# A four-layer hybrid decoder on one core: the first mixer's gate work moved one slot, more buffers, and its constants and first squares moved ahead

## The reference, cut to what matters

```python
def _rg_lru_mixer(h, w_in, conv_w, conv_b, w_gate, b_gate, lam, w_out):
    bsz, s, _ = h.shape
    proj = h @ w_in
    gate_branch, xr = proj[..., :D_RNN], proj[..., D_RNN:]
    xc = _causal_dwconv(xr, conv_w, conv_b)
    xb = xc.reshape(bsz, s, LRU_BLOCKS, LRU_BLK)
    gates = (jnp.einsum('bsnc,nce->bsne', xb, w_gate) + b_gate).astype(jnp.float32)
    r = jax.nn.sigmoid(gates[..., :LRU_BLK]).reshape(bsz, s, D_RNN)
    i = jax.nn.sigmoid(gates[..., LRU_BLK:]).reshape(bsz, s, D_RNN)
    log_a = -LRU_C * r * jax.nn.softplus(-lam.astype(jnp.float32))
    a = jnp.exp(log_a)
    u = jnp.sqrt(-jnp.expm1(2.0 * log_a)) * (i * xc.astype(jnp.float32))
    _, hs = lax.associative_scan(_linear_combine, (a, u), axis=1)
    y = jax.nn.gelu(gate_branch.astype(jnp.float32)) * hs
    return y.astype(h.dtype) @ w_out
```

## Time and profile before

| | us |
|---|---|
| median of three runs (1874.1 to 1875.57) | 1874.65 |
| the profiled execution | 1872.53 |
| its span, first to last instruction | 1870.7 |
| mean granted clock of TensorE, as a share | 0.988 |

### The profile page before, as it was taken

One profiled execution on the slowest core, in us unless ns is written; L12 is line 12 of the kernel. 1 busy time (PEld: TensorE's weight loads), 2 busy tenths in 40 slices (PEclk: granted clock), 3 DMA queues, 4 the chain that ended last, 5 costly groups with the idle time before them and its releaser, 6 DMA issues.

```text
span 1870.7 us, 25413 instructions
## 1 busy us (share of the span) xinstructions
PE 1798.5 (96%) x8912; PEld 1131.2 (60%) x8912; DVE 1194.5 (64%) x1971; ACT 1143.2 (61%) x1601; POOL 1178.1 (63%) x1678
## 2 busy tenths in 40 slices
PE   6989999999999898999999999999999999999999
PEld 3545666655655555666666776666657777566665
DVE  6775777327877853777416875777137777577730
ACT  6876666557776745766545667666443545676642
POOL 4545877876354436777886307777875445478785
PEclk9999999999999998999999999999999999999999
DMA  5314444444223223444443103444442222244443
GB/s 203 109 57 147 136 154 143 153 148 129 80 79 91 80 68 113 157 147 147 145 157 115 58 2 119 151 147 141 160 133 90 81 89 76 83 150 144 152 155 120
DMA packets 64926, 224.80 MB, mean 120 GB/s; under 512 B 7328, under 2 KB 8864, under 8 KB 64544
## 3 DMA queue, kind: packets, MB, share of 16 engines
q1 hardware_dynamic: 64224, 221.69, 36.4%
q10 hardware_dynamic: 576, 1.49, 0.2%
HBM read 221.05 MB, written 2.10 MB: 119 GB/s over the span
## 4 chain that ended last, share of the span: by engine, by line
PE 78%; ACT 9%; DVE 9%; issue 3%; DMA 0%; POOL 0%; DVEq 0%; SPq 0%; ACTq 0%
PE psum L274 22%; PE psum L284 21%; PE psum L316 12%; PE psum L320 11%; PE psum L1657 3%; ACT w_big L232 2%; PE psum L1239 1%; PE psum L2051 1%; DVE psum L1463 1%; PE psum L2034 1%; PE psum L2070 1%; ACT x_big L342 1%; PE psum L1228 1%; ACT psum L1328 1%; ACT psum L346 1%
## 5 line engine op out<-in xcount | busy, mean ns | idle before, releaser
L248 POOL TENSOR_TENSOR w_rest<-w_panel,w_big 128x256 bf16<-128x256 f32 (+1 forms) x1674 | 1177.9, 742 | 679.7 <-ACT w_big L232 679.6
L274 PE MATMUL psum<-x_big,w_big 128*128 128x512 f32 x2248 | 662.8, 428 | 14.9 <-ACT x_big L342 14.3
L284 PE MATMUL psum<-x_rest,w_rest 128*128 128x512 bf16 x2248 | 556.8, 383 | 1.4 <-POOL w_rest L248 1.4
L232 ACT ACTIVATE w_big<-w_panel 128x1024 fp32r<-128x1024 f32 (+3 forms) x425 | 422.3, 1018 | 171.6 <-PE psum L320 93.2
L274 PEld LDWEIGHTS psum<-x_big,w_big 128*128 128x128 f32 x2248 | 420.0, 190 | 138.6 <-issue 20.0
L284 PEld LDWEIGHTS psum<-x_rest,w_rest 128*128 128x128 bf16 x2248 | 189.6, 98 | 284.2 <-issue 106.8
L605 DVE SCALAR_TENSOR_TENSOR psum<-ffn_raw,params,psum 128x512 f32<-128x512 f32 x352 | 264.5, 752 | 7.2 <-ACT psum L559 1.0
L597 DVE TENSOR_TENSOR ffn_raw<-psum,rstd 128x512 f32<-128x512 f32 x176 | 121.3, 691 | 141.2 <-PE psum L284 121.2
L559 ACT ACTIVATE psum<-ffn_raw,params 128x512 f32<-128x512 f32 x176 | 137.4, 782 | 101.5 <-DVE ffn_raw L597 101.3
L316 PE MATMUL psum<-g_big,w_big 128*128 128x512 f32 x704 | 199.3, 423 | 0.0
L451 DVE SCALAR_TENSOR_TENSOR x_resid<-psum,x_resid 128x512 f32<-128x512 f32 x64 | 43.8, 688 | 227.8 <-PE psum L320 227.7
(11 more groups left out here) (251 smaller groups left out, 1831.5 us busy)
## 6 DMA issues: line engine op xcount, KB each, us to landing
w_panel<-in_up SPq DMA_DIRECT2D x176, 512.0 KB, 3.4
w_panel<-in_dn SPq DMA_DIRECT2D x64, 448.0 KB, 3.1
w_panel<-in_ssd_in SPq DMA_DIRECT2D x41, 512.0 KB, 3.5
w_panel<-in_dn SPq DMA_DIRECT2D x32, 512.0 KB, 3.4
w_panel<-in_hgrn_in SPq DMA_DIRECT2D x32, 512.0 KB, 3.5
w_panel<-in_lru_in SPq DMA_DIRECT2D x19, 512.0 KB, 3.4
w_panel<-in_ssd_out SPq DMA_DIRECT2D x16, 512.0 KB, 3.5
w_panel<-in_swa_in SPq DMA_DIRECT2D x12, 512.0 KB, 3.5
```

The costliest lines, as they stand in the source:

```text
L232: act.activation(k.w1[:, slot, lo:words], k.w[:, slot, lo:words], ACT.Copy, scale=(SHIFT - 1) / SHIFT).then_inc(k.s("panel_big"), 1)
L248: rest = pool.tensor_tensor(k.w2[:, slot, a], k.w[:, slot, a], k.w1[:, slot, a].bitcast(F32), ALU.subtract)
L274: pe.matmul(out, k.w1[:, slot, q * m:(q + 1) * m], k.x1[:, q, :], start=q == 0, stop=False)
L284: mm = pe.matmul(out, k.w2[:, slot, q * m:(q + 1) * m], k.x2[:, q, :], start=False, stop=q == DT - 1)
```

## The change

- **The queues of the units.** The inner and GELU steps of unit j move into slot j+1, as `inner(j - 1)` and `gelu(j - 1)` on VectorE and `gelu(j - 1)` on ScalarE. ScalarE's square of gate j stays in slot j, at its end, ahead of the root, which now stands at the end of the even slots. `rest` moves from slot j+3 to slot j+4, right behind `raw`. `gates(0)` on TensorE comes ahead of gate tile 1.
- **Buffers.** `a`, `root` and `wu` have four, with waits on unit j-4. The order of the bank releases changes accordingly, and `release` says which comes when.
- **The last two units.** After slot 9 the steps of units 8 and 9 alternate, the y of unit 9 stands in bank 5, and `lru_step` counts the steps in the new order. TensorE takes unit 6, then unit 7, into the early output tiles before it waits for all ten.
- **Softplus.** `lru_lambda` is loaded with the first small DMA. The chain begins ahead of the tiles of x and ends behind them, before the units; two of its buffers are now in PSUM.
- **The head.** The squares of x tiles 1 to 5 are done by GpSimd, in two pieces of 128x256 each, ahead of its panels (the rest of panel 0 comes behind the first square). ScalarE runs an exponential on a dummy as its first operation. It rounds panel 1 before the norm and panel 2 behind it; before, it rounded panels 1 and 2 ahead of the norm.

```diff
+POOL_SQUARES = range(1, 6)
...
+def release(g):
+    if g >= 2 * LRU_T:
+        return g
+    j = g // 2
+    return min(g + 1, 2 * LRU_T - 1) if g % 2 else max(g - 1, 0)
@@ first_scalar
+    act.wait_ge(k.s("banks_free"), 4)
+    act.activation(b.t4, k.rstd[:, 0:LRU_T], ACT.Exp)
...
         scaled_x(act, k, 0, o)
-        square_x(act, k, 0, o)
-    round_until(act, k, 2)
+        if o == 0:
+            square_x(act, k, 0, o)
+            softplus_scalar(act, k, "lru_softplus", b.t3, b.t1)
+        elif o not in POOL_SQUARES:
+            square_x(act, k, 0, o)
+    round_until(act, k, 1)
+def first_squares(pool, k):
+    for o in POOL_SQUARES:
+        pool.wait_ge(k.s(f"x{o}_landed"), 16)
+        if o >= 3:
+            pool.wait_ge(k.s("sq_summed"), o - 2)
+        for half in range(2):
+            at = slice(half * PIECE, (half + 1) * PIECE)
+            sq = pool.tensor_tensor(k.sq[:, o % 2, at], k.x[:, o, at], k.x[:, o, at], ALU.mult)
+        sq.then_inc(k.s("x_squared_pool"), 1)
+        if o == 1:
+            weights_gpsimd(pool, k, 0)
@@ first_vector, behind the loop over the tiles of x
+    lru_softplus_end(dve, k, softplus)
@@ LruBuffers
-        self.conv, self.a, self.root, self.wu = (a.take(2, S) for _ in range(4))
+        self.conv = a.take(2, S)
+        self.a, self.root, self.wu = (a.take(4, S) for _ in range(3))
@@ lru_y
-    return k.ps[:, 7 if j % 2 else 4, :]
+    return k.ps[:, 5 if j == LRU_T - 1 else 7 if j % 2 else 4, :]
@@ lru_tensor
-        if j > 1:
-            gates(j - 1)
+        gates(j - 1)
         project(gate_tile(j))
-        if j == 1:
-            gates(0)
-    pe.wait_ge(k.s("lru_y_split"), LRU_BEGUN - 2)
-    out_steps(pe, k, "lru_out", 0, 0, LRU_BEGUN - 2, k.y1, k.y2)
+    out(0, 0, LRU_BEGUN - 2)
     gates(LRU_T - 1)
...
+    out(1, 0, LRU_BEGUN - 2)
+    for o in (2, 3):
+        out(o, 0, LRU_BEGUN - 1)
+    for o in (0, 1):
+        out(o, LRU_BEGUN - 2, LRU_BEGUN - 1)
+    for o in range(OUT_EARLY["lru_out"]):
+        out(o, LRU_BEGUN - 1, LRU_BEGUN)
@@ lru_scalar
+    for j in range(LRU_T):
+        bias(j)
+        round_ahead(act, k, job, raw_tile(j))
+        if j:
+            gates(j - 1)
+            decay(j - 1)
+        round_ahead(act, k, job, gate_tile(j))
+        if j:
+            gelu(j - 1)
+        if j >= 3:
+            high(j - 3)
+        square(j)
+        if j >= 2 and j % 2 == 0:
+            root(j - 2)
+    gates(LRU_T - 1)
+    decay(LRU_T - 1)
+    gelu(LRU_T - 1)
+    root(LRU_T - 2)
+    for j in range(LRU_T - 3, LRU_T):
+        high(j)
@@ lru_vector
+    for j in range(LRU_T):
+        mid, old = j >= 1, j >= 3
+        raw(j)
+        if j >= 4:
+            rest(j - 4)
+        tap(j, 0)
         if old:
             rooted(j - 3)
+        tap(j, 1)
         if old:
             driven(j - 3)
+        tap(j, 2)
         if old:
             scan(j - 3)
+        if mid:
+            gated(j - 1)
+            inner(j - 1)
         if old:
             joined(j - 3)
+        gate(j)
         if mid:
+            gelu(j - 1)
+    six, seven, eight, nine = range(LRU_T - 4, LRU_T)
+    rest(six)
+    inner(nine)
+    rooted(seven)
+    gated(nine)
+    driven(seven)
+    gelu(nine)
+    scan(seven)
+    joined(seven)
+    rooted(eight)
+    rooted(nine)
+    driven(eight)
+    driven(nine)
+    rest(seven)
+    scan(eight)
+    scan(nine)
+    joined(eight)
+    joined(nine)
+    rest(eight)
+    rest(nine)
```

More of the change, by code:

```diff
@@ L393, in sum_squares @@
         return
-    dve.wait_ge(k.s("x_squared"), DT * c + o + 1)
+    if c == 0 and o in POOL_SQUARES:
+        dve.wait_ge(k.s("x_squared_pool"), o)
+    else:
+        dve.wait_ge(k.s("x_squared"), x_squared(c, o))
     if o > 1:
@@ L685, in __init__ @@
         self.half_bias = a.take(2 * LRU_T)
-        self.nlam, self.t0, self.t1, self.t2, self.t3 = (a.take(LRU_T) for _ in range(5))
+        self.nlam, self.t0, self.t1, self.t2, self.t3, self.t4 = (a.take(LRU_T) for _ in range(6))
         self.gate_w = a.take(LRU_T * 256)
```

134 lines of the change are left out of this document (57 added, 77 removed).

## The result

The changed kernel takes 1850.99 us (median of four runs, 1850.15 to 1851.29), against 1874.38 for the kernel before, measured beside it (four runs, 1873.68 to 1875.57). The ratio is 0.9874, with a 95% interval from 0.9857 to 0.9891: 23.4 us won, where 22.6 were forecast. The profiled execution took 1850.15 us with a span of 1848.3, and the mean granted clock was 0.994 instead of 0.988.

The account below looks back on a forecast made before the run. TensorE, busy for 96% of the span, was taken as the bound, with VectorE and ScalarE waiting for each other inside mixer units; 2.5 + 6.7 + 7.8 + 5.6 = 22.6 us off 1874.65 gave 1852.0, range 1848.5 to 1861.0.

Parts of the forecast that it names:

- head, to unit 0: Start of the kernel: squares on GpSimd and an earlier table load start unit 0 at 24.5 against 26.98, 2.5 us.
- units 0 to 2: First mixer units: softplus chain out of slot 0, gates(0) ahead of gate tile 1; 22.9 us instead of 29.6, 6.7 won.
- units 3 to 8: Middle mixer units: reordered queues give 8.9 us even, 10.5 odd slots; 56.8 us against 64.6, 7.8 won.
- tail: From unit 9's start to the last rest: 24.1 us instead of 29.7, 5.6 us won.
- output tiles: Behind the last rest: 24.9 us that hang on the last high, which keeps its place; they stay.
- late next: Odd slots: the bias queued behind ScalarE's table load and root starts 2.35 us behind raw, so the slot takes 10.5 us.
- Slow squares: Head: GpSimd needs 1.46 us a piece, squares 2 to 5 end 5.8 us later, 1857.8 us; chance 0.12.
- The pair stays: Mixer units: reordering only moves the stall, table loads and bias wait remain, 7.8 us not won, 1859.8; chance 0.12.
- The clock: Unit gates: new TensorE idles halve its clock, 2.6 us each, 28.6 us in all, 1880.6; chance 0.03.
- The shared port: Seven units: GpSimd's pieces come before VectorE's rooted, which loses up to 0.73 us each, 5.1 us, 1857.1; chance 0.08.

Follow-up runs that it names:

- doubled squares: Changed kernel with GpSimd making each of its five squares of x tiles twice, the first copy to spare memory: 1854.57 us, ratio 0.9895.
- late softplus: Changed kernel with the end of the softplus chain back in VectorE's slot 0, behind the eviction of gate 0: 1851.69 us, ratio 0.9882.
- panel 2 first: Changed kernel with panel 2 rounded ahead of the norm again, nothing else moved: 1851.87 us, ratio 0.9873.
- root's table removed: Changed kernel with a copy of the same shape in place of the square root, so the units need no table loads: 1848.80 us, ratio 0.9862.
- bias moved: Changed kernel with the bias of units 5, 7 and 9 on VectorE instead of ScalarE: 1847.37 us, ratio 0.9852.
- GELU in its own slot: Changed kernel with inner, gelu and bank release back in the unit's own slot, gated and rest in old places, four buffers kept: 1864.86 us, ratio 0.9946.
- serial tail: Changed kernel with units 8 and 9 one after the other on VectorE instead of alternating: 1852.17 us, ratio 0.9877.

## Why the prediction was right, step by step

The walk through the queues carried it. The forecast of 1852.0 lies between the two medians of the changed kernel, 1850.99 and 1852.74, so the last microsecond of the agreement means nothing. Its five terms, each from the traces of before and of the changed kernel:

| step | forecast | measured |
|---|---|---|
| head, to unit 0 | 2.5 | 26.98 - 24.25 = 2.7 |
| units 0 to 2 | 6.7 | 29.57 - 23.57 = 6.0 |
| units 3 to 8 | 7.8 | 64.61 - 56.34 = 8.3 |
| tail | 5.6 | 29.73 - 23.96 = 5.8 |
| output tiles | 0 | -0.1 to 0.1 |
| sum, to the FFN | 22.6 | 22.7 |

*Head.* The total was right, one of its reasons was wrong, and two errors covered each other. I had priced a piece of a square at 0.73 us and called GpSimd's squares the pace of the head. The source line's summary in the changed kernel (ns, least, median, most):

```profile
L415 POOL TENSOR_TENSOR x_sq<-x_resid x10: 608/620/1161, 7.2 to 14.5; 128x256 f32<-128x256 f32 x10
```

The eight pieces of squares 2 to 5 take 4.62 us together, 0.58 each, and end at 15.14 where I had 16.2. The pace is ScalarE's: two operations for a tile, 1.23 us apart from 8.97 on, with no idle between them. The doubled squares show how near GpSimd is behind. The last sum ended at 18.4 instead of 19.4, but in TensorE's queue the sum over features stands behind the remainders of tile 0, eight matmuls in 3.64 us from 16.97, and started at 20.40. So raw 0 came at 24.25, almost as forecast (24.5).

*Units 0 to 2* were over-estimated by 0.7 us. The walk had the queues of the changed kernel right; what it named as the reasons of the gain, the chain out of slot 0 and `gates(0)` ahead, is in part not borne out and in part not shown, as said with the late softplus. The wait for panel 2 was forecast at 0.7 and is 0.80. Unit 1 came at 30.01 (forecast 29.6), and units 1 and 2 took the 8.9 us of the walk. The term was mis-sized by its start: 0.4 us in unit 1, and unit 0's own 0.25. The moved rounding is the cause of the wait, as the run with panel 2 first shows. The run with the late softplus shows that the chain, as short as it now is (4.1 us), may stand in either place.

*Units 3 to 8* were under-estimated by 0.5 us: even units took 8.8 to 8.9 us (forecast 8.9), odd ones 10.41 and 10.48 (10.5), and unit 3 took 8.91 instead of 9.1. The forecast's own two parts of an even unit, 8.1 and 0.7 us, add up to 8.8, which is what units 6 and 8 took (8.82). What was named as late next was late: the bias stood 2.32 us behind raw (2.35), and the runs with the root's table removed and with the bias moved each gave the time back.

*Tail and output tiles.* 23.96 against 24.1, in the order foreseen: scan 7 from 118.41 (forecast 104.2 + 14.3 = 118.5). The output tiles stayed at 24.6.

The rivals. *Slow squares* fell with the 0.58 us. The Trainium skill, GPSIMD Engine Reference, "Elementwise — side-by-side cycle accounting", says that GpSimd takes about twice VectorE's time. No run has the squares on VectorE, but its operations of this size in the head lie 0.60 us apart, and 1.16 us a square is 1.9 times that, so the trace agrees. ScalarE's queue gave up 0.52 us a square. It was still right to use GpSimd, since it was idle. *The pair stays* was right about what remained (two table loads, the bias) and wrong that nothing would be won. *The clock* did not fall: the granted clock was 1.00, 2.4 GHz, from its first record at 20.54 us to the FFN, and behind unit 0 the matmuls ran at that rate, with TensorE idle for 0.65 and 0.43 us in unit 8 and for 1.49, 1.28 and 1.24 us in and behind the tail. Before, an idle of 1.98 us was followed by 0.50, and in the run with the GELU in its own slot idles of up to 2.1 us came back, with 0.92 in unit 5. It was not far off in the tail: with the serial tail TensorE stood idle for 2.00 us ahead of 128.29, where the changed kernel has 1.28, and the trace has 0.50 from 128.59 on. It cost nothing there, since the output tiles still took 24.67 us.

*The shared port* shows, but was small. `rooted` took 692 to 766 ns in all ten units; in unit 4 it starts at 58.93, 0.36 us ahead of GpSimd's pieces, so it comes first, as in the walk. The other side paid. GpSimd's group of four pieces beside it and one that runs clear of it:

```profile
59.29 2.99 POOL L258 TENSOR_TENSOR w_rest<-w_panel,w_big 128x256 bf16<-128x256 f32 x4 [1.24 <-ACT w_big L242]
63.18 2.80 POOL L258 TENSOR_TENSOR w_rest<-w_panel,w_big 128x256 bf16<-128x256 f32 x4 [0.90 <-ACT w_big L242]
```

0.19 us are lost by GpSimd, where it has over 1 us to spare. The head has a clearer case. In the changed kernel the first square started at 7.16, beside VectorE's first remainder of the weights at 7.17, which has both operands in SBUF:

```profile
7.16 1.73 POOL L415 TENSOR_TENSOR x_sq<-x_resid 128x256 f32<-128x256 f32 x2 [6.72 <-DMA x_resid<-in_x]
7.17 0.68 DVE L273 TENSOR_TENSOR w_rest<-w_panel,w_big 128x512 bf16<-128x512 f32 x1
```

In the second execution of the same kernel, where the tile of x landed 1.6 us earlier, the two don't meet, and the same line reads:

```profile
L415 POOL TENSOR_TENSOR x_sq<-x_resid x10: 610/612/613, 5.6 to 14.3; 128x256 f32<-128x256 f32 x10
```

One piece grew from 0.61 to 1.16 us, by 0.55, most of VectorE's 0.68. It can fall on VectorE too. In the run with the late softplus the remainder of the weights started 0.05 us behind a square's piece (7.03 us), the piece kept its 0.61 us, and VectorE's line reads:

```profile
7.08 1.11 DVE L273 TENSOR_TENSOR w_rest<-w_panel,w_big 128x512 bf16<-128x512 f32 x1
```

The Trainium skill, SBUF — State Buffer, "SBUF: two separate sides", says that whichever of the two starts first has the shared pair of ports for its whole instruction, and the other stands still. The late softplus agrees: VectorE came second and waited. The changed kernel shows the standing still too, but its two starts are less than 0.01 us apart, and it was GpSimd, with the earlier start, that paid, so this pair doesn't tell the order.

## What to carry to other kernels

When two engines wait for each other inside a loop step, moving one of the two chains a step later removes the wait, but in full only together with the buffers that let it be late: of 8.3 us in units 3 to 8 the buffers alone won nothing here, and the order alone 3.5. Walk each engine's queue with durations from the trace until one engine is full in each kind of step; what that engine does ahead of its first handed-over result (here a table load and a root ahead of a bias) is the next thing to move. Check the stretches between markers, not the total, for edits below the scatter of executions.

## What the runs showed that was not expected

**A product with float32 result is faster on GpSimd than a subtraction with bfloat16 result**, over the same 256 elements: 0.58 us against 0.69 from start to start (2.77 to 2.80 us for four). The squares also read one operand twice, so the runs don't tell whether the result type, the operation or the single source makes the difference.

**TensorE is slow in the head, where the profile shows a clock of 1.00, and for how long varies.** The remainders of tile 0 and the sum over features in three executions: the changed kernel, its second run, and the run with the late softplus, whose head is the same up to here:

```profile
16.97 3.64 PE L294 MATMUL psum<-x_rest,w_rest 128*128 128x512 bf16 x8
...
20.40 1.09 PE L535 MATMUL psum<-x_sqsum,consts 128*128 128x512 f32 x2
```

```profile
16.78 3.09 PE L294 MATMUL psum<-x_rest,w_rest 128*128 128x512 bf16 x8
...
19.70 1.02 PE L535 MATMUL psum<-x_sqsum,consts 128*128 128x512 f32 x2
```

```profile
17.32 3.64 PE L294 MATMUL psum<-x_rest,w_rest 128*128 128x512 bf16 x8
...
20.75 1.91 PE L535 MATMUL psum<-x_sqsum,consts 128*128 128x512 f32 x2
```

The same groups take 1.90 and 1.02 us elsewhere at the high clock, so 3.64 and 1.91 are what 1.2 instead of 2.4 GHz gives, while the busy times by stretch show a clock of 1.00 in each microsecond of all three. That 1.00 is not a reading. The traces hold clock records only from 20.54, 19.17 and 22.64 us on, all three at 1.00, and these are just the times at which the matmuls get fast. So ahead of the first record the spacing of the matmuls is to be read, and not the clock. Why the first record comes when it does the rows don't say; ahead of it TensorE had been idle for 0.95 us, and for about half of the time since 5 us. In the second run the speed changes inside the first group, in the first one between the two, and in the third one behind both. Unit 0 hangs on this sum, and comes 8.06, 8.64 and 9.45 us behind the last high part of x. That is why the run with the late softplus starts late, and it is one part of the scatter.

**The landing of one panel is a second part, and the clock behind it a third.** From the FFN's start to the end of the span the traces have 1694.3 to 1700.3 us for the same instructions. At the FFN's start ScalarE's queue holds the rounding of a panel ahead of its scaling of the last tile of x, and so TensorE waits for a load. The chain of the changed kernel has it:

```profile
149.17 5.00 DMA w_panel<-in_up
...
154.25 1.06 ACT w_big L242
155.30 0.62 ACT x_big L352
```

The load took 5.0 us, where the median of this queue's loads is 3.4. The wait ahead of the rounding was 0.28 us in the kernel before, 0.16 in the second run of the changed kernel, 1.82 here, and 3.15 in the run with panel 2 first, whose gain it hid. TensorE itself stood still for 0, 0, 1.27 and 2.64 us. It was not tried to put the rounding behind the scaling. That leaves over 4 us of the spread, and the clock goes with it: behind the FFN's start it stands at 0.50 for 20.5 us in all in both traces of the changed kernel (1694.3 and 1695.0 us without TensorE's wait), for 27.3 us with the root's table removed (1696.9), and for 30.7 us with the late softplus (1698.5). What makes the clock fall more often in one execution than in another is not shown.
